# Folding the combining stage of a mixture-of-experts layer into its expert tiles, on one Trainium2 core

## The reference, cut to what matters

```python
def hier_moe(h, ...):
    g_idx = argmax(t @ w_rg + b_rg)                      # one group of 4
    e_in  = (expert logits)[:, g_idx]                    # the 4 experts of that group
    top_v, top_i = top_k(e_in, 2)
    top_w = softmax(top_v) * g_w
    hid = silu(t @ w_gate[e]) * (t @ w_up[e])            # 1024 -> 256, for both experts e
    return sum over both of (hid * top_w) @ w_down[e]    # 256 -> 1024

h2 = rms_norm(x) * (1 + sc2) + sh2
x  = x + g2 * hier_moe(h2)                               # g2: one row for prompt, one for sample
```

## Time and profile before

| | |
|---|---|
| median of 3 runs | 1586.67 us (1586.63 to 1588.01) |
| the profiled execution: from its first to its last instruction (span) | 1585.9 us |
| that execution's own time outside the span | not shown; the median lies 0.8 us above the span |
| PE busy | 1376.0 us (87%) |
| DVE busy | 770.6 us (49%) |
| ACT busy | 458.6 us (29%) |
| POOL busy | 178.2 us (11%) |
| DMA, mean over the span | 130 GB/s |

### The profile page before, as it was taken

The page is one execution under the profiler, slowest core; times in us unless marked ns, Lnnn a source line. Parts: engine busy times, 40 slices in busy tenths (PEclk is TensorE's granted clock), DMA queues, the critical chain, the costliest instruction groups (busy, mean ns, idle before and its releaser), DMA issues. The chain is left out here.

```text
span 1585.9 us, 20591 instructions
## 1 busy us (share of the span) xinstructions
PE 1376.0 (87%) x7461; PEld 798.6 (50%) x7462; DVE 770.6 (49%) x1683; ACT 458.6 (29%) x989; POOL 178.2 (11%) x366
## 2 busy tenths in 40 slices
PE   3899997979999899999689998899943999999960
PEld 2555553656644566666456665544423454444430
DVE  0421224868496798889755563423344111111118
ACT  3321112232455466663235551011110111111110
POOL 0000002022010111112100000000001223222220
PEclk9999997989989999999899999999975999999985
DMA  8400016752131442230130003522348468775728
GB/s 323 170 3 4 31 51 156 220 174 31 26 86 38 143 133 74 69 124 29 64 131 1 1 1 142 169 97 86 113 143 298 156 219 276 262 272 196 264 95 321
DMA packets 138826, 205.85 MB, mean 130 GB/s; under 512 B 27205, under 2 KB 102917, under 8 KB 138533
## 3 DMA queue, kind: packets, MB, share of 16 engines
q1 hardware_dynamic: 122524, 160.08, 30.9%
q0 software_dynamic: 10272, 32.49, 5.7%
q10 hardware_dynamic: 5946, 12.15, 2.3%
HBM read 158.71 MB, written 43.98 MB: 128 GB/s over the span
## 5 line engine op out<-in xcount | busy, mean ns | idle before, releaser
L2233 PE MATMUL ps<-ex_wgu,ex_xT 128*128 x416 | 185.1, 598 | 4.0 <-ACT ex_xT L2272 2.5
L1390 DVE TENSOR_SCALAR_CACHE_REDUCE tk_eq<-sc,tk_cand 128x512 bf16<-128x512 f32 (+4 forms) x155 | 146.8, 1007 | 0.0
L2233 PEld LDWEIGHTS ps<-ex_wgu,ex_xT 128*128 128x128 f32 x416 | 77.8, 192 | 93.1 <-issue 93.1
L1788 PE MATMUL ps<-hT,mergedT 128*128 128x512 f32 (+1 forms) x288 | 120.1, 600 | 4.9 <-DMA op_wr<-in_w_route_expert 4.9
L1324 PE MATMUL ps<-zT,gt_w 128*128 128x352 f32 (+1 forms) x384 | 120.9, 468 | 0.0
L1324 PE MATMUL ps<-hT,gt_w 128*128 128x352 f32 (+1 forms) x336 | 105.8, 468 | 0.0
L2306 DVE SCALAR_TENSOR_TENSOR ex_hid<-ex_silu,ex_weight,ps 128x256 f32<-128x256 f32 x26 | 12.5, 480 | 185.0 <-ACT ex_silu L2278 185.0
L1324 PEld LDWEIGHTS ps<-zT,gt_w 128*128 128x128 f32 x384 | 73.0, 190 | 44.1
L2254 PE MATMUL ps<-ex_wd,ex_hidT 128*128 x208 | 93.6, 593 | 0.2 <-DVE ex_hidT L2313 0.2
L1353 ACT ACTIVATE mask<-sc,tk_cand 128x384 bf16<-128x384 f32 (+1 forms) x62 | 82.3, 1329 | 15.0 <-DVE tk_cand L1406 15.0
L1788 PEld LDWEIGHTS ps<-hT,mergedT 128*128 128x128 f32 (+1 forms) x288 | 50.9, 186 | 68.4 <-issue 62.7
(11 more groups left out here) (468 smaller groups left out, 2134.1 us busy)
## 6 DMA issues: line engine op xcount, KB each, us to landing
ex_wgu<-in_w_gate SPq DMA_DIRECT2D x16, 1024.0 KB
ex_wgu<-in_w_up SPq DMA_DIRECT2D x16, 1024.0 KB
ex_wd<-in_w_down SPq DMA_DIRECT2D x16, 1024.0 KB
sp_ada_w<-in_w_ada SPq DMA_DIRECT2D x9, 1024.0 KB
cb_y<-y_dram ACTq DMA_DIRECT2D x16, 512.0 KB, 7.6
merge_left_dram<-qiT SPq DMA_DIRECT2D x8, 544.0 KB, 6.1
mg_gb<-gate_b_dram SPq DMA_DIRECT2D x8, 544.0 KB, 3.8
mergedT<-merge_left_dram SPq DMA_DIRECT2D x8, 544.0 KB, 4.7
```

What stands on the lines that cost most here:

```text
L1390: return v.tensor_scalar(junk[j], m.sc[0:r, c:c + w], scalar, 0.0, op, ALU.add, accum_out=cnt[0:r, j:j + 1])
L1788: i = nc.tensor.matmul(m.ps[rows, 2 * (t % 2) + n, :], m.mergedT[:, k, t * P:t * P + r], m.wout[:, k, n * 512:(n + 1) * 512], start=k == 0 ...
L2233: j = nc.tensor.matmul(m.ps[:, 2 + b, :], xT[:, b, k, :], wgu[:, bass.ds(at, 1), k, :].rearrange("p o n -> p (o n)"), start=k == 0, stop=k ...
```

## The change

The experts run in another order: place e of the order holds expert e % 4 * 4 + e // 4, so the first experts of all four groups come first, then all second ones, and so on (`expert_at`; `routing` counts in that order). A token's two experts are of one group, so they stand at least four experts, and thus four tiles, apart.

`combine`, `y_dram` and the loads of the residual rows are gone. Instead each tile gathers the rows of `x1_dram` of its own tokens (`gather_sum`), multiplies the result of `down` by the gate on DVE (`gated`), adds the gathered rows (`added`) and scatters (`scatter`): a token's earlier tile writes the sum back to `x1_dram`, its later tile writes to the output. For that there are two indirect DMAs with a bound for each tile; a row number past the bound (`SKIP` is added to it) isn't written. The sample's rows always go back to `x1_dram`, and SP copies them to the output after the last scatter.

Before a tile's rows are gathered, all scatters of the iteration before must have landed (`ys`). The gate row of each slot is made on DVE (`gate_rows`). `routing` makes the new table columns (earlier or later, prompt or sample).

```diff
+def expert_at(e):
+    return e % NG * EPG + e // NG
...
+                step(v.tensor_copy(tok[:, :, :], toki[:, :, :]))
+                for c, one in enumerate((oh1, oh2)):
+                    step(tt(e2, one, bc(iota[:, 0:EPG], 1, TILES), ALU.mult))
+                    step(v.tensor_reduce(when[:, c, :], e2, AX.X, ALU.add))
+                for c in range(2):
+                    step(tt(when[:, 2 + c, :], when[:, c, :], when[:, 1 - c, :], ALU.is_gt))
+                    step(v.scalar_tensor_tensor(tok[:, 1 + c, :], when[:, 2 + c, :], float(NT), tok[:, 1 + c, :], ALU.mult, ALU.add))
...
                 dve.wait_ge(tp, 1)
-                step(v.tensor_copy(m.by_slot[:, :, 0:MAXT], m.ps[:, 2, 0:3 * MAXT].rearrange("p (a n) -> p a n", a=3)))
-                rows = m.by_slot[:, 1, 0:MAXT]
-                step(ts(none[:, :], rows, 0.0, None, ALU.is_equal))
-                step(tt(none[:, :], none[:, :], spare[:, :], ALU.mult))
-                step(v.scalar_tensor_tensor(rows, rows, -1.0, none[:, :], ALU.add, ALU.add))
+                token = m.ps[:, 2, 0:MAXT]
+                step(v.tensor_copy(m.slot_ints[:, 0:MAXT, 0], token))
...
+                    step(ts(stays, stays, -float(SKIP), float(SKIP), ALU.mult, ALU.add))
+                    step(tt(m.slot_ints[:, 0:MAXT, j], stays, token, ALU.add))
...
-                for t in range(TILES):
-                    sp.dma_start(m.x1[t][0:rows_of(t), :], m.x1_dram[t * P:t * P + rows_of(t), :]).then_inc(m.x1l, 16)
...
+                sp.wait_ge(all_done, 1)
+                sp.dma_start(O.y_sample[0, :, :], m.x1_dram[SEQ:NT, :]).then_inc(sample_stored, 16)
...
+                def gather_sum(i, b):
+                    n = 2 * i + b
+                    wait(pool, ys[0], 32 * i)
+                    wait(pool, ys[1], 32 * i)
+                    nc.gpsimd.tensor_copy(row[:, b, :], m.slot_ints[:, bass.ds(n, 1), :].rearrange("p o n -> p (o n)")).then_inc(rc, 1)
+                    wait_alone(3 + b, rc, n + 1)
+                    nc.gpsimd.indirect_dma_start(
+                        out=acc[:, b, :], out_offset=None, in_=m.x1_dram,
+                        in_offset=bass.IndirectOffsetOnAxis(ap=row[:, b, 0:1], axis=0)).then_inc(al[b], 16)
...
+                    wait_alone(5 + b, yr, n + 1)
+                    if b == 0:
+                        wait_alone(8, al[1], 16 * i + 16)
+                    for j, dst, rows in ((1, m.x1_dram, NT), (2, O.y_prompt[0, :, :], SEQ)):
+                        nc.gpsimd.indirect_dma_start(
+                            out=dst, out_offset=bass.IndirectOffsetOnAxis(ap=row[:, b, j:j + 1], axis=0),
+                            in_=yo[:, b, :], in_offset=None, bounds_check=rows - 1, oob_is_err=False).then_inc(ys[b], 16)
...
                 def body(i):
-                    for b in range(2):
-                        gather(i + 1, b)
-                        previous(scatter, i, b)
-                        weights(i + 1, b)
+                    previous(scatter, i, 0)
+                    gather(i + 1, 1)
+                    weights(i + 1, 0)
+                    gather_sum(i, 0)
+                    gather_sum(i, 1)
+                    scatter(i, 0)
+                    gather(i + 2, 0)
+                    weights(i + 1, 1)
...
+                def gate_rows(i, b):
+                    v.scalar_tensor_tensor(gate[:, b, :], m.gate2[:, 0, 1, :], wcol[:, b, 1:2], m.gate2[:, 0, 0, :],
+                                           ALU.mult, ALU.add).then_inc(gr, 1)
...
+                def gated(i, b):
+                    n = 2 * i + b
+                    wait(dve, ys[b], 32 * i)
+                    dve.wait_ge(gr, n + 1)
+                    dve.wait_ge(dn, n + 1)
+                    v.tensor_tensor(yo[:, b, :].rearrange("p (c n) -> p c n", c=2), m.ps[:, 4:6, :],
+                                    gate[:, b, :].rearrange("p (c n) -> p c n", c=2), ALU.mult).then_inc(yg, 1)
...
+                def added(i, b):
+                    n = 2 * i + b
+                    dve.wait_ge(yg, n + 1)
+                    dve.wait_ge(al[b], 16 * i + 16)
+                    v.tensor_tensor(yo[:, b, :], yo[:, b, :], acc[:, b, :], ALU.add).then_inc(yr, 1)
...
                 def body(i):
                     for b in range(2):
                         hidden(i, b)
-                        previous(rows, i, b)
+                        gate_rows(i, b)
+                        previous(gated, i, b)
                         hidden_copy(i, b)
+                        previous(added, i, b)
                         xts(i + 1, b)
```

More of the change, by code:

```diff
@@ L2079, in _, with experts @@
                 step(ts(m.loops[:, 1:2], m.loops[:, 0:1], -1.0, None, ALU.add))
-                step(v.memset(m.by_slot[:, :, MAXT:], 0.0))
+                step(v.memset(m.slot_ints[:, MAXT:, :], 0))
+                step(v.memset(m.slot_floats[:, MAXT:, :], 0.0))
+                early, late, sample, kept, out, t1 = (own[:, j, :] for j in range(6))
                 dve.wait_ge(tp, 1)
-                step(v.tensor_copy(m.by_slot[:, :, 0:MAXT], m.ps[:, 2, 0:3 * MAXT].rearrange("p (a n) -> p a n", a=3)))
-                rows = m.by_slot[:, 1, 0:MAXT]
-                step(ts(none[:, :], rows, 0.0, None, ALU.is_equal))
-                step(tt(none[:, :], none[:, :], spare[:, :], ALU.mult))
-                step(v.scalar_tensor_tensor(rows, rows, -1.0, none[:, :], ALU.add, ALU.add))
-def experts(nc, m, A):
+                token = m.ps[:, 2, 0:MAXT]
+                step(v.tensor_copy(m.slot_ints[:, 0:MAXT, 0], token))
+                step(v.tensor_copy(m.slot_floats[:, 0:MAXT, 0], m.ps[:, 2, 2 * MAXT:3 * MAXT]))
+                step(v.tensor_copy(code[:, :], m.ps[:, 2, MAXT:2 * MAXT]))
+                step(ts(late, code[:, :], float(NT), None, ALU.is_gt))
+                step(ts(early, code[:, :], 0.0, None, ALU.is_gt))
+                step(tt(early, early, late, ALU.subtract))
+                step(ts(sample, token, float(SEQ), None, ALU.is_ge))
+                step(v.tensor_copy(m.slot_floats[:, 0:MAXT, 1], sample))
+                step(tt(kept, early, sample, ALU.max))
+                step(tt(t1, late, sample, ALU.mult))
+                step(tt(out, late, t1, ALU.subtract))
+                for j, stays in ((1, kept), (2, out)):
+                    step(ts(stays, stays, -float(SKIP), float(SKIP), ALU.mult, ALU.add))
+                    step(tt(m.slot_ints[:, 0:MAXT, j], stays, token, ALU.add))
+def experts(nc, m, A, O):
     LOOPS = (-(-2 * NT // P) + 1) // 2, MAXT // 2
@@ L2177, in scatter @@
                 def scatter(i, b):
                     n = 2 * i + b
[L2179 to L2186, removed]
@@ L2197, in before @@
                         weights(0, b)
+                    gather(1, 0)
                 def after(last):
@@ L2201, in after @@
                     for b in range(2):
-                        pool.wait_ge(ys[b], 16 * last + 16)
-                        pool.wait_ge(gl[b], 16 * last + 32)
+                        pool.wait_ge(ys[b], 32 * last + 32)
+                        pool.wait_ge(gl[b], 16 * last + (48, 32)[b])
+                    nc.gpsimd.tensor_tensor(idle[:, 7:8], idle[:, 0:1], idle[:, 0:1], ALU.add).then_inc(all_done, 1)
                 nc.gpsimd.memset(idle[:, 0:1], 0.0).then_inc(idle_set, 1)
@@ L2249, in down @@
                     pe.wait_ge(htc, n + 1)
-                    wait(pe, yea, n)
-                    wait(pe, yed, n)
+                    wait(pe, yg, n)
                     for c in range(2):
@@ L2278, in silu @@
                     nc.scalar.activation(sl[:, b, :], m.ps[:, 2 + b, 0:FD], ACT.Silu).then_inc(slr, 1)
-                def rows(i, b):
-                    wait(act, ys[b], 16 * i)
-                    act.wait_ge(dn, 2 * i + b + 1)
-                    nc.scalar.copy(yo[:, b, 0:512], m.ps[:, 4, :]).then_inc(yea, 1)
                 def body(i):
@@ L2287, in body @@
                         silu(i, b)
-                        previous(rows, i, b)
                         xts(i + 1, b)
-                run(act, body, lambda: (xts(0, 0), xts(0, 1)), lambda last: rows(last, 1))
+                run(act, body, lambda: (xts(0, 0), xts(0, 1)))
             @block.vector
@@ L2371, in fresh_semaphores @@
+                v.tensor_tensor(m.gate2[:, 0, 1, :], m.gate2[:, 0, 1, :], m.gate2[:, 0, 0, :], ALU.subtract).then_inc(dg, 1)
+                dve.wait_ge(dg, 1)
+                run(dve, body, lambda: (xts(0, 0), xts(0, 1)), lambda last: (gated(last, 1), added(last, 1)))
 def fresh_semaphores(nc, m):
@@ L2465, in program @@
         with nc.sbuf_tensor("ex_wgu", [P, RING, KD, 2 * FD], F32) as m.wgu, nc.sbuf_tensor("ex_wd", [P, RING, 2, D], F32) as m.wd:
-            m.x1 = [flat(m.hT)[:, t * D:(t + 1) * D] for t in range(PT)] + [flat(m.zT)[:, 0:D]]
-            m.x1l = m.sem("x1_loaded")
             m.wl = [m.sem(f"ex_weights_loaded{i}") for i in range(RING)]
             routing(nc, m, A)
-            experts(nc, m, A)
```

(2 more changed lines are left out.)

104 lines of the change are left out of this document (34 added, 70 removed).

## The result

The changed kernel takes 1599.0 us, the median of 4 runs (1597.6 to 1602.5), against 1586.65 (1584.2 to 1588.0) for the kernel before on the same chip: a ratio of 1.0076 with a 95% interval of 1.0060 to 1.0093, some 12 us **slower**. The forecast was 1575, faster; its range of 1549 to 1609 held the time. The profiled execution has a span of 1600.7 us, and was already 1.3 us late at the start of routing (DVE's first L2014 step at 1181.00 us before, the same step, L2023, at 1182.33 after).

A forecast was written before the change was run, and what follows sets the result against it. It took PE's tiles and the 52.3 us behind PE's last matmul as the bound. PE's end 1533.6 + 3.8 - 4.5 + (15 + 10 + 4) = 1561.9, + 12.5 = 1574.4, median 0.8 above: 1575 us, range 1549 to 1609.

The forecast's parts named there:

- the ring of waits on POOL: Expert loop: scatter, sums, next scatter, input rows and PE's tiles take 48.1 us per two iterations against PE's 45.6.
- POOL's longest waits would be at the landings: Sign of being right: POOL waits longest for landings of scatters and sums, no longer at the result rows.
- the term of the loop: Expert loop: ring 2.5 us too long per two iterations, six times, 15 us, with landings of 4.5, 5.7 and 5.7.
- rival 1: Expert loop: PE stays the bound, landings sum to 13.4 or less, at most 5 us lost; 1546 to 1556; chance 0.18.
- Rival 2: Expert loop: landings meet weight loads, sum 20.1, 68 us lost, 1614 us; chance 0.30 together with rival 3.
- Its break-even of 18.4 us: Expert loop: landings summing to about 18.4 us, 6.1 each, from which the change comes out slower.
- The clock: Expert loop: after each stall PE runs at clock 0.50 for 3.4 us, losing 1.7; six times, 10 us.
- DVE beside POOL: Expert loop: two-input DVE operations delay POOL's steps, up to 1.29 us per pair, 8 in all; 4 taken.
- The tail: Behind PE's last matmul: 52.3 us go; last sum, scatter and sample's copy take their place, together 12.5 us.
- Routing and start: Before the first `gate_up`: new DVE routing steps cost 3.8 us; without residual-row loads PE starts 4.5 us earlier.
- Rival 3: Expert loop: bounded scatter's instruction takes 1.5 us, not 1.01; 9 us more, 1584; chance 0.30 together with rival 2.

The follow-up runs named there:

- e11: Changed kernel with both input-row gathers issued earlier (ahead of the sums' gathers and of the iteration's first scatter), DRAIN kept: 1550.7 us, ratio 0.9772.
- e7: Changed kernel without the weight loads of the last 13 experts, all waits and POOL work kept: 1560.9 us, ratio 0.981.
- e4: Changed kernel without `gate_rows`, every row multiplied by the prompt's gate: 1592.6 us, ratio 1.0042.
- e2: Changed kernel without POOL's DRAIN at the end of the expert block: 1596.4 us, ratio 1.0056.
- e8: Changed kernel with a DRAIN on POOL at the end of each expert loop iteration: 1601.8 us, ratio 1.0089.
- e1: Changed kernel with the input-row gather for the first tile two iterations on moved ahead of the sums' gathers: 1576.8 us, ratio 0.9933.

## Why the prediction was wrong, point by point

- **Where to look** was right: the ring of waits on POOL, with the gather of the input rows behind the scatter, is the cause. e11 undoes just that, and the loop is back at PE's own pace. The stalls came where the prediction looked for them, at even tiles in every other iteration. Its sign that POOL's longest waits would be at the landings did not come: they were for DVE's sums (148.2 us). Removing the combining stage pays, as argued.
- **The step that failed** is the term of the loop, "this ring is 2.5 us too long for each two iterations", six times, 15 us, and in it the landings. It gave one set of them (4.5 + 5.7 + 5.7 = 15.9 us) to all iterations. There were five long stalls of 3.3 to 6.0 us. In their rings the landings sum to 16.2 to 20.7, on average 18.3. The count of the ring itself was right: with the landings as measured it gives 24.4 us for the five together, and PE waited 25.1 (27.8 with the three short waits); for a single ring it is off by up to 1.9. Stalls don't average: a short ring gives nothing back for a long one. By the medians after, 13.2, rival 1 (no stall) would have held.
- **Rival 2** is what happened, in some of the iterations: landings that meet the weight loads, as e7 shows. Its break-even of 18.4 us was for six equal rings; two of the five pass it, and their mean of 18.3 lies just under it. Its 6.5 to 6.8 us for each landing stood in the earlier trace rows; they were read as a case for all iterations or for none, when they are one for those that meet a load.
- **The clock**: 10 us predicted, 11.8 measured, in stretches of 3.4 to 10.2 us at 0.50 that begin in the five longer stalls. That the sums are near is in part luck: six times 1.7 us was predicted, five times 2.4 came.
- **What was left out of the loop**: some 4 us more ahead of `gate_up` than before (7.7 in the two rows against 4.0), by the sequencer's lost lead, and about 4 us of longer work that isn't clock. e7 has such longer work too (304.8 us busy at a granted clock of 0.99, against 300.1), and many short pauses as well; its cause stays open.
- **DVE beside POOL**: 4 us predicted; about 5 by e4, not clear of noise. The prediction had the full size as 8 us, and POOL's steps are stretched by 8.1. In the row above POOL's instruction starts 0.19 us into a DVE operation of 1.28 and lasts 0.97 longer than its median. That is nearly all of what was left of it, as the Trainium skill (SBUF — State Buffer, "Who interferes with whom") says of a GpSimd instruction that reads SBUF. `added`, which also has two inputs in SBUF, does the same: in e11 three gathers of input rows, issued 0.2 us into it, take 1.88 or 1.89 us where 1.0 is usual. One of them:

```profile
1402.14 1.22 DVE L2369 TENSOR_TENSOR ex_y<-ex_y,hT 128x1024 f32<-128x1024 f32 x1
1402.36 1.88 POOL L2198 DMA_INDIRECT ex_x<-h_dram,ex_idx  x1 [0.15 <-issue]
```

- **The tail**: 12.5 us predicted, 17.6 measured. Without the DRAIN it is 11.9 in e2, so the terms were about right (they add up to 12.7, not 12.5); the DRAIN was missing. The kernel before had one of 4.47 us behind the expert block, which the prediction didn't look up.
- **Routing and start**: +3.8 predicted; POOL starts the expert stage at 1219.2 us where it started at 1213.7, 5.5 later, less the 1.3 from earlier stages: +4.2. From the second gather's issue to `gate_up` it took 10.94 us before (1217.36 to 1228.30) and takes 6.74 now (1222.88 to 1229.62): -4.2 for the -4.5 predicted.
- **Rival 3** fell: the bounded scatters' instructions take 1.00 and 0.98 us.
- The misses sum up: loop 19.2 + tail 5.1 + routing and start 0.7 + earlier stages 1.3, less 2.5 for a median 1.7 below the span where 0.8 above it was assumed, is 23.8 of the 24.0 us between 1575 and 1599.

## What to carry to other kernels

Count a ring of waits with the landings of the worst stretch as well as with the medians, and ask in which iterations the transfers meet others; a ring that fits on average can still stall PE, and the longer stalls (3.3 us and more here) cost clock on top. Before that, look at what stands in a queue behind a wait that it has no need of: here two lines moved ahead of it were worth 48 us. And leave PE's sequencer its lead: where a branch and register loads stand behind the transposes, as here, the rows should land 1.4 us before the transposes could start.

## What the runs showed of the hardware

- A DRAIN on POOL at the end of a block takes time for the indirect DMAs issued since the last one, even with all of them landed: 4.47 us after 54, 9.06 after 107, so 83 and 85 ns each, and 0.46 after 2, as much as POOL's DRAIN of the routing block (L1970) took after none. Leaving it out where semaphores cover the transfers gained 4.8, 6.2 and 7.6 us in three comparisons; in the first of them the time went to the next block's DRAIN, off the path. What it does in that time wasn't tried. With a gather in flight, the DRAINs of e8 lasted until 0.4 us after its landing (4.8 to 8.9 us).
- In e1 PE's sequencer took 1.8 us from the start of the register load of `tile_place` to the first matmul of `gate_up` (1454.6 to 1456.4), and this is hidden only while it runs ahead of the engine. A landing 0.1 to 0.8 us ahead of the transposes showed as no wait at them and as 0.66 to 1.23 us ahead of the `gate_up` behind them, with a releaser that is none.
- An indirect DMA's instruction on POOL that starts inside a DVE operation with two inputs in SBUF is stretched by nearly what is left of that operation: 1.95 us in place of 0.99 beside `gate_rows`, 1.88 in place of 1.0 beside `added`.
